# Latent heads: the rotation moved from VectorE to GpSimd, and part of the norm weight applied by ScalarE's copies

## What is computed

```python
q = (rms_norm(c_q, q_a_norm) @ w_uq).reshape(B, S, MLA_HEADS, MLA_QK_DIM)      # 8 heads of 96
kv = (rms_norm(c_kv, kv_a_norm) @ w_ukv).reshape(B, S, MLA_HEADS, MLA_NOPE_DIM + MLA_V_DIM)
k = jnp.concatenate([k_nope, broadcast(k_rope)], axis=-1)                      # 64 + 32
q = rms_norm(q, q_norm)
k = rms_norm(k, k_norm)
q = jnp.concatenate([q[..., :MLA_NOPE_DIM], apply_rope(q[..., MLA_NOPE_DIM:], pos)], axis=-1)
k = jnp.concatenate([k[..., :MLA_NOPE_DIM], apply_rope(k[..., MLA_NOPE_DIM:], pos)], axis=-1)
```

## Time and profile before

| | us |
|---|---|
| median of 3 runs | 2205.34 (2203.54 to 2207.75) |
| the profiled execution | 2202.24 |
| its span | 2200.4 |
| PE busy | 1979.2 (90%) |
| DVE busy | 951.5 (43%) |
| ACT busy | 701.0 (32%) |
| POOL busy | 457.3 (21%) |

### The profile page before, as it was taken

The page is one execution under the profiler, slowest core; times in us unless marked ns, Lnnn a source line. Parts: engine busy times, 40 slices in busy tenths (PEclk is TensorE's granted clock), DMA queues, the critical chain, the costliest instruction groups (busy, mean ns, idle before and its releaser), DMA issues. The chain is left out here.

```text
span 2200.4 us, 30381 instructions
## 1 busy us (share of the span) xinstructions
PE 1979.2 (90%) x11293; PEld 1263.0 (57%) x11293; DVE 951.5 (43%) x2308; ACT 701.0 (32%) x1765; POOL 457.3 (21%) x619
## 2 busy tenths in 40 slices
PE   6999859999999998959999768999999999999887
PEld 3444435655587665645655535666666557766664
DVE  3896974433261211114223486666665125321111
ACT  4013554531111111112122475767666111111110
POOL 0001002331022222100000264445445001222111
PEclk8999969999989999979999988999999999999998
DMA  5000001132588999862000200001000515999992
GB/s 220 0 0 0 0 16 52 36 94 109 211 315 305 375 376 364 307 215 43 1 0 1 80 1 11 11 11 49 11 11 20 195 68 197 340 360 379 377 356 75
DMA packets 80889, 307.78 MB, mean 140 GB/s; under 512 B 18352, under 2 KB 23495, under 8 KB 63846
## 3 DMA queue, kind: packets, MB, share of 16 engines
q1 hardware_dynamic: 66342, 272.23, 32.2%
q0 software_dynamic: 14400, 33.59, 6.2%
HBM read 276.75 MB, written 47.89 MB: 148 GB/s over the span
## 5 line engine op out<-in xcount | busy, mean ns | idle before, releaser
L1112 POOL TENSOR_SCALAR nsaatt_probs<-nsaatt_probs,nsaatt_inv,trunk_gates_or_logits 128x384 f32<-128x384 f32 (+7 forms) x256 | 185.6, 739 | 202.1 <-DVE nsaatt_inv L1139 202.1
L1125 DVE CUSTOM_DVE_ANT_0 nsaatt_probs<-nsaatt_scores,trunk_arena 128x384 f32<-128x384 f32 (+7 forms) x256 | 151.3, 629 | 87.8 <-PE nsaatt_scores L1031 87.5
L1761 DVE TENSOR_TENSOR experts_sig<-experts_gu_ps,experts_sig 128x256 f32<-128x256 f32 x50 | 21.2, 425 | 356.2 <-ACT experts_sig L1718 356.2
L1083 ACT ACTIVATE nsaatt_probs<-nsaatt_probs,nsaatt_bias 128x384 f32<-128x384 f32 (+7 forms) x256 | 169.0, 667 | 11.8 <-DVE nsaatt_bias L1134 11.7
L1594 PEld LDWEIGHTS experts_gu_ps<-experts_x_cols,ahead 128*128 128x128 f32 x1408 | 159.1, 192 | 8.9 <-issue 8.9
L1594 PE MATMUL experts_gu_ps<-experts_x_cols,ahead 128*128 128x128 f32 x1408 | 161.6, 276 | 2.8 <-ACT experts_x_cols L1713 2.8
L1031 PE MATMUL nsaatt_scores<-layer_k_cols,trunk_x_rows 64*128 64x384 f32 (+3 forms) x640 | 131.1, 521 | 15.7 <-DVE nsaatt_top L1125 12.8
L1041 PE MATMUL nsaatt_turn<-trunk_ident,nsaatt_probs 128*128 128x128 f32 x912 | 123.8, 279 | 23.5 <-POOL nsaatt_probs L1112 6.0
L1718 ACT ACTIVATE experts_sig<-experts_gu_ps 128x256 f32<-128x256 f32 x50 | 19.2, 383 | 369.3 <-PE experts_gu_ps L1594 242.5
L1041 PEld LDWEIGHTS nsaatt_turn<-trunk_ident,nsaatt_probs 128*128 128x128 f32 x912 | 97.3, 140 | 57.4 <-issue 37.7
L2239 PE MATMUL nsain_q_ps<-trunk_arena,l1b_h_cols 128*128 128x512 f32 x256 | 111.7, 594 | 0.0
(11 more groups left out here) (444 smaller groups left out, 3804.2 us busy)
## 6 DMA issues: line engine op xcount, KB each, us to landing
ahead<-in_moe_w_gate_dram SPq DMA_DIRECT2D x34, 1024.0 KB, 14.3
ahead<-in_moe_w_up_dram SPq DMA_DIRECT2D x34, 1024.0 KB, 20.8
ahead<-in_moe_w_down_dram SPq DMA_DIRECT2D x34, 1024.0 KB, 22.1
trunk_arena<-in_moe_w_gate_dram SPq DMA_DIRECT2D x10, 1024.0 KB, 14.0
trunk_arena<-in_moe_w_up_dram SPq DMA_DIRECT2D x10, 1024.0 KB, 18.5
trunk_arena<-in_moe_w_down_dram SPq DMA_DIRECT2D x10, 1024.0 KB, 25.9
moe_w<-in_moe_w_gate_dram SPq DMA_DIRECT2D x10, 1024.0 KB, 12.5
moe_w<-in_moe_w_up_dram SPq DMA_DIRECT2D x10, 1024.0 KB, 23.4
```

Source lines behind the costliest of these rows:

```text
L1083: act.activation(part(s, r, h), part(s, r, h), ACT.Exp, bias=bias[:, b, i:i + 1], scale=steps[s]["scale"][h], accum_out=total[:, b, i:i + ...
L1112: pool.tensor_scalar(part(s, r, h), part(s, r, h), inv[:, s % BUFS, i:i + 1], 1.0 if gate is None else gate[h], ALU.mult, ALU.mult).then_i ...
L1125: dve.tensor_tensor_reduce(part(s, r, h), scores_of(s, r, h), br["mask"], 1.0, -3e38, ALU.add, ALU.max, top[:, s % BUFS, i:i + 1]).then_in ...
```

## The change

- DVE's `rotate` becomes `scale`: the multiplication by the root stays, the norm weight is applied on DVE only to the 32 rotary dimensions of each head (two multiplications of 128x256).
- The rotation, the same six instructions, is made by POOL, in its own queue: rotate(t-2) ahead of the copy of the key part of tile t, the last two behind the loop. POOL signals `qk_ready`.
- A column tensor `gain_cols` holds the norm weights of the other 64 dimensions, one column for queries and one for keys, and 1.0 in the 32 rotary rows. ACT's copies behind the transposition take it as their scale.
- Two more loads fill `gain_cols`, 64 single elements each, and DVE sets its last 32 rows to 1.0 at the start of the stage.

```diff
-    HERE = 16 * 4
+    HERE = 16 * 6
...
+                def rotate(t):
+                    b = t % 2
+                    x1, x2 = qk[:, b, :, NOPE:NOPE + HALF], qk[:, b, :, NOPE + HALF:]
+                    rot = sq[:, b].rearrange("p h d -> p (h d)")[:, 0:4 * HEADS2 * HALF].rearrange(
+                        "p (n h d) -> p n h d", n=4, h=HEADS2)
+                    c, s = (over(m[:, t:t + 1, :], (P, HEADS2, HALF)) for m in (cos, sin))
+                    pool.wait_ge(scaled, 3 * (t + 1))
+                    for n, (x, m) in enumerate(((x1, c), (x2, s), (x1, s), (x2, c))):
+                        pool.tensor_tensor(rot[:, n], x, m, ALU.mult).then_inc(rotated, 1)
+                    pool.wait_ge(rotated, 6 * t + 4)
+                    pool.tensor_tensor(x1, rot[:, 0], rot[:, 1], ALU.subtract).then_inc(rotated, 1)
+                    pool.tensor_tensor(x2, rot[:, 2], rot[:, 3], ALU.add).then_inc(rotated, 1)
+                    pool.wait_ge(rotated, 6 * (t + 1))
+                    pool.engine_nop().then_inc(qk_ready, 1)
+
                 for t in range(TILES):
                     if t >= 2:
+                        rotate(t - 2)
                         pool.wait_ge(turned, GROUPS * (t - 1))
...
+                rotate(TILES - 2)
+                rotate(TILES - 1)
...
                 def columns(t):
+                    if t == 0:
+                        act.wait_ge(here, HERE)
+                        act.wait_ge(gain_ready, 1)
                     for g in range(GROUPS):
                         n = GROUPS * t + g
+                        side = g // (GROUPS // 2)
                         act.wait_ge(turned, n + 1)
                         act.activation(head_columns(n), turn[n % 2][0:QK, :].rearrange("p (h n) -> p h n", h=4),
-                                       ACT.Copy).then_inc(out_act, 1)
+                                       ACT.Copy, scale=gain_cols[0:QK, side:side + 1]).then_inc(out_act, 1)
...
-                def rotate(t):
+                def scale(t):
                     b = t % 2
-                    steps = 9 * t
                     dve.wait_ge(rstd_ready, t + 1)
                     rows = qk[:, b]
                     dve.tensor_tensor(rows, rows, over(rstd[:, b, :].unsqueeze(2), (P, HEADS2, QK)), ALU.mult).then_inc(scaled, 1)
-                    dve.wait_ge(scaled, steps + 1)
+                    dve.wait_ge(scaled, 3 * t + 1)
                     for side in range(2):
-                        half = qk[:, b, side * MLA_HEADS:(side + 1) * MLA_HEADS, :]
-                        dve.tensor_tensor(half, half, over(qk_gain[:, side:side + 1, :], (P, MLA_HEADS, QK)), ALU.mult).then_inc(scaled, 1)
...
+                        rope = qk[:, b, side * MLA_HEADS:(side + 1) * MLA_HEADS, NOPE:]
+                        dve.tensor_tensor(rope, rope, over(qk_gain[:, side:side + 1, NOPE:], (P, MLA_HEADS, ROPE)), ALU.mult).then_inc(scaled, 1)
...
+                dve.memset(gain_cols[NOPE:QK, :], 1.0).then_inc(gain_ready, 1)
...
+                with nc.allow_non_contiguous_dma(reason="small, once"):
+                    for side, norm in enumerate(("mla_q_norm", "mla_k_norm")):
+                        sp.dma_start(gain_cols[0:NOPE, side:side + 1],
+                                     A[norm][0][0:NOPE].rearrange("(d o) -> d o", o=1)).then_inc(mla_here, 16)
```

More of the change, by code:

```diff
@@ L619, in mla_inputs @@
 def mla_inputs(nc, latents, lat_sum, q_cols, k_cols, v_rows, conv, gated, taps, conv_bias, conv_out_cols, ln_g, ln_b,
-               w_uq, w_ukv, lat_gain, qk_gain, here, sin, cos, causal, ident, ones):
+               w_uq, w_ukv, lat_gain, qk_gain, gain_cols, here, sin, cos, causal, ident, ones):
     HEADS2 = 2 * MLA_HEADS
@@ L650, in mla_inputs @@
              "centred", "conv_squared", "conv_own", "conv_mean", "conv_rooted", "conv_scaled", "affine", "conv_sig"))
-        pe_tapped = ph.sem("pe_tapped")
+        pe_tapped, rotated, gain_ready = ph.sem("pe_tapped"), ph.sem("rotated"), ph.sem("gain_ready")
         GROUPS = HEADS2 // 4
@@ L869, in rotate @@
                     dve.tensor_tensor(rows, rows, over(rstd[:, b, :].unsqueeze(2), (P, HEADS2, QK)), ALU.mult).then_inc(scaled, 1)
-                    dve.wait_ge(scaled, steps + 1)
+                    dve.wait_ge(scaled, 3 * t + 1)
                     for side in range(2):
-                        half = qk[:, b, side * MLA_HEADS:(side + 1) * MLA_HEADS, :]
-                        dve.tensor_tensor(half, half, over(qk_gain[:, side:side + 1, :], (P, MLA_HEADS, QK)), ALU.mult).then_inc(scaled, 1)
[L874 to L880, removed]
-                    dve.wait_ge(scaled, steps + 7)
-                    dve.tensor_tensor(x1, rot[:, 0], rot[:, 1], ALU.subtract).then_inc(scaled, 1)
-                    dve.tensor_tensor(x2, rot[:, 2], rot[:, 3], ALU.add).then_inc(scaled, 1)
-                    dve.wait_ge(scaled, steps + 9)
-                    dve.engine_nop().then_inc(qk_ready, 1)
+                        rope = qk[:, b, side * MLA_HEADS:(side + 1) * MLA_HEADS, NOPE:]
+                        dve.tensor_tensor(rope, rope, over(qk_gain[:, side:side + 1, NOPE:], (P, MLA_HEADS, ROPE)), ALU.mult).then_inc(scaled, 1)
                 def tap(j):
@@ L934, in _ @@
                         conv_variance(t - 5)
-                    rotate(t)
+                    scale(t)
                     if t < 4:
@@ L2963, in layer0 @@
             qk_gain = inner.sb("qk_gain", [P, 2, QK])
+            gain_cols = inner.sb("gain_cols", [P, 2])
             taps = inner.sb("taps", [P, CONV_TILES, TAPS])
@@ L2991, in layer0 @@
             mla_inputs(nc, latents, lat_sum, q_cols, k_cols, v_rows, conv, gated, taps, conv_bias, conv_cols, ln_g, ln_b,
-                       w_uq, w_ukv, lat_gain, qk_gain, mla_here, sin, cos, causal, ident, ones)
+                       w_uq, w_ukv, lat_gain, qk_gain, gain_cols, mla_here, sin, cos, causal, ident, ones)
         out_w = ph.sb("out_w", [P, CHUNKS, BANK])
```

## The result

The changed kernel takes 2213.22 us (median of 5 runs, 2210.47 to 2217.14); the kernel before, beside it, 2205.34. The ratio is 1.0037, with a 95% interval of 1.002 to 1.0055: slower by 7.9 us. The profiled execution took 2213.22 (span 2211.5).

A forecast was written before the change was run, and what follows sets the result against it. VectorE (DVE) paces the stage, a dependent loop close behind with 2.0 us of slack. Interval terms +0.8, +0.4, +1.6, +3.2, 0, -1.1, +3.7, +0.4 sum to +9.0 on the median 2205.34: 2214.3 us, range 2202 to 2225.

The forecast's parts named there:

- The sign and its place: Query/key stage: slower, through the loop from scaling over GpSimd's rotation to ACT's root; chance of over 0.2% slower 0.68.
- The price of 0.72: GpSimd's rotation: each 128x256 instruction takes 0.72 us, 4.3 for six; bounds 0.64 and 0.82.
- The plain loop: Scaling 2.5, tap in front 1.2, six ops 4.3, own waits 0.3, transposition to root 3.7: 12.0 us a tile.
- Interval 0: Between the first two starts of DVE's root multiplication: 12.6 against 11.80, +0.8, with half a chance of another tap.
- Interval 3: Fourth to fifth root multiplication: rotation, transposition, PE's sums and centring without slack, 19.6 against 16.39, +3.2.
- Interval 5: Sixth to seventh root multiplication: DVE's four products take turns with four rotation ops, 13.3 against 14.36, -1.1.
- Interval 6: Seventh to eighth root multiplication: 13.3 plus 1.2 for PE's lower clock, 14.5 against 10.80, +3.7.
- That all of it reaches the end: Stage's end: a barrier, attention starts straight after, so all +9.0 us shows in the kernel's time.
- 1: Plain loop: GpSimd and DVE don't obstruct each other, loop 10.8, -2.6, 2202.7; chance 0.20 together with rival 4.
- 2: Loop from scaling to root: no obstruction as in rival 1, and ops at 0.64; -5.5, 2199.8; chance 0.10.
- 3: PE's transpositions: clock falls from the second tile on, six more 1.2 longer each, +7 on top, 2221; chance 0.14.
- 4: DVE keeps its length, as taps and products wait for GpSimd; time within 4 us; chance 0.20 together with rival 1.

The follow-up runs named there:

- second pair: The kernels before and after the change, unedited, each profiled a second time; 2205.33 and 2211.18 us, one run each.
- e2: Changed kernel with the whole norm weight on DVE again and plain ACT copies, rotation still on GpSimd; 2217.84 us, 1.006 of the kernel before.
- e1: Changed kernel with the rotation back on DVE, ACT's scaled copies kept; 2202.98 us, 0.999 of the kernel before.
- e6: Kernel before with the four taps behind the rotation made ahead of the loop; 2201.66 us, 0.9982 of the kernel before.
- e9: Changed kernel with rotation on DVE, PE's taps cut from 12 to 10, 13 DVE taps ahead of the loop; 2198.53 us, 0.9973 of before.
- e3: Changed kernel with the four taps behind the scaling made ahead of the loop; 2210.55 us, 1.0022 of the kernel before.
- e4: Changed kernel with plain ACT copies, norm weight of the 64 unrotated dimensions left out; 2210.78 us, 1.0023 of the kernel before.
- e11: Kernel before with four taps ahead of the loop and unread PE products during waits for the last two tiles' transpositions; 2200.64 us, 0.9978.

## Why the prediction was right, and where it wasn't

**The sign and its place: right.** The stage after the change is a loop from scaling over GpSimd, PE and ACT back to scaling, where it had been DVE's sum. The signs that I named are there: 0.73 an instruction, a first one of 1.71 (named: 1.9), DVE waiting for the root, interval 6 at 13.15, and copies of 0.63 to 0.68 (named: 0.69). The starts are 11.52 us apart where I had named 12, just above the 11.5 below which I would have called it wrong. GpSimd's busy time rose by 43.2 (named: 45). DVE's fell by 19.9, not 27: its records hold the waits for GpSimd's turns, 1.6 in each of two groups of L923 (4.10 less 2.49), and about 2 more in the last products (L961).

**The price of 0.72: right.** 0.73 recorded, 0.69 from start to start, between the 0.64 by size alone and the 0.82 that was my high end. The Trainium skill's ratio of 1.96 (GPSIMD Engine Reference, "Elementwise — side-by-side cycle accounting") I had put on DVE's recorded length, 0.42, for an estimate of 0.8, and that was too dear: recorded, GpSimd's is 1.7 times DVE's. From start to start it is 0.69 against 0.34, 2.0 times, so there this trace agrees with the page's ratio.

**The sum: right in sign, too large in the stage.** I had +9.0; both pairs of profiles show +5.4 (140.36 less 135.00, 140.11 less 134.67). By interval, in us:

| interval | 0 | 1 | 2 | 3 | 4 | 5 | 6 | 7 |
|---|---|---|---|---|---|---|---|---|
| forecast | +0.8 | +0.4 | +1.6 | +3.2 | 0 | -1.1 | +3.7 | +0.4 |
| measured, first pair | -0.21 | -0.06 | +1.14 | +3.01 | -0.06 | -1.00 | +2.35 | +0.18 |

In the second pair intervals 0, 3 and 6 are +0.37, +2.27 and +2.64. The two loads, which I had put at nothing, cost nothing that these show: the stage starts at 191.03 and 190.44 in the kernel before, at 191.86 and 190.40 in the kernel after.

- The plain loop was 11.52, not 12.0. Of that 0.48, 0.36 lies in the rotation (5.44 against 5.8): the six instructions follow each other at 0.69, and the two waits on itself cost about 0.1 each. The rest is the scaling (2.47) and the way to the root (3.61).
- Interval 0: the second tap that I gave half a chance (0.6) did not come between GpSimd's instructions, as DVE's next work there is the reduction, which waited 1.56 us for the squares. In e2, whose scaling is longer, it did come.
- Interval 3: the rotation with its tap and the sum beside it took 6.41 (forecast 7.0), the transpositions 3.72 (3.0): the granted clock from 258 to 262 was 0.50. Two errors of opposite sign.
- Interval 5: the rotation beside four products of DVE, from 292.35 to 298.52, took 6.2, where I had added 2.5, 4.3 and 0.3, together 7.1. Turns cost less than the sum of both, since one pair goes by in 1.14 where 0.62 and 0.69 are 1.31. But the way from rotation to the next scaling was 4.8 and not 3.7, at the lower clock. Here too the two errors are of opposite sign, and that the interval came out right is luck.
- Interval 6: the same 6.2 instead of 7.1, and 4.5 for the way back, where I had 3.7 and 1.2 for the lower clock. Both errors have the same sign here, so this was the largest single error, 1.3, and most of it is the price of the turns and not the clock.

**That all of it reaches the end: right, but something else went with it.** Stage and opening together are 160.35 before and 167.84 after, +7.5, against +7.9 between the medians; in the second pair +5.9 (165.80 against 159.87) against 5.85 between the times of those two profiled executions. The spans of the first two profiled executions are 11.1 apart; 0.8 of that lies ahead of the stage and 2.8 behind the opening, in parts that the change doesn't touch, so two executions can differ by 3 us or more without it. The experiments follow roughly, stage with opening first and then time: e1 -3.2 and -2.6, e6 -3.9 and -4.0, e9 -6.8 and -5.6, e2 +13.4 and +12.2, e3 +3.6 and +4.9; worst is e4, +2.7 and +5.1. So it is partly luck that the total of 2214.3 came within 1.1 of the median: a stage oversized by 3.6 met an opening that I had not priced, +2.1 in the first pair and only +0.5 in the second.

**The rivals.** 1 and 2 (no turns) fell with the 1.71, and e3 shows what they would have had beside the taps: 1.0 less an interval, and still slower than before. Turns beside the layer norm's products are left in e3, so it tests these rivals only in intervals 0 to 3. 3 (the clock falls from the second tile on): in the middle it was 0.94 against 0.97, and tiles 1 and 2 were transposed at full speed (1.08 and 1.22 for eight); it came true for tiles 3 and 5, where 16 took 3.80 and 3.81 and the kernel before had 1.08 for the first eight. In the second profile the second eight of tile 0 took 1.76, too. 4 (DVE keeps its length) holds for a quarter of the 27 us, 7.1, and the time did not stay.

## What to carry to other kernels

Before work is moved off the busiest engine, find the dependent loop that runs just behind it: here it left two microseconds of slack for any saving on that engine, and the work moved was itself a link of that loop, at twice the time from start to start. Try each half of such a change alone, since here one half was worth -2.6 us and the other +10.5. And when the first limit moves, ask which engine is next (PE, at 10.5 us a tile): with four taps already out of the way, the copies' half was worth nothing in intervals 0 to 2 until two of PE's taps were moved as well, and then 3.1 us.

## What was not expected of the hardware

- GpSimd and DVE in turns, a pair of products at 1.14 us where each alone takes 0.69 and 0.62: a part of each, some 0.17 in all, overlaps.
- The granted clock fell to 0.51 from 342 to 354 with PE busy 10.97 of 12 us, and in the second profile of the same kernel only until 350 (0.53 from 344 to 350, 1.00 from 350 to 356). In e11 it was 0.64 from 334 to 346 with PE busy all 12 us. The same program's time can thus differ by 2 us at a place the change never touched.
- Not every busy neighbour costs something: while DVE reduced from 232.59 to 234.34 (one input in SBUF), GpSimd's instructions kept their 0.73.
